# A chunked linear-attention step: the score tiles of the prompt heads reduced from eight to six

## What is computed

```python
def step(s, inp):                                   # one chunk of tokens, one state s per head
    qb, kb, vb, gb = inp
    G = jnp.cumsum(gb, axis=1)                      # log decay, per token and channel
    o_inter = jnp.einsum('bthk,bhkv->bthv', qb * jnp.exp(G), s)
    decay = jnp.exp(jnp.where(causal, G[:, :, None] - G[:, None, :], -jnp.inf))
    scores = jnp.einsum('bthk,btshk->btsh', qb, decay * kb[:, None])
    o_intra = jnp.einsum('btsh,bshv->bthv', scores, vb)
    ...
```

## Time and profile before

| | us |
|---|---|
| time, median of three runs | 1828.41 |
| the three runs | 1827.68, 1828.41, 1837.21 |
| the profiled execution, its own time | 1836.97 |
| its span (first to last instruction) | 1835.2 |

### The profile page before, as it was taken

How to read it: one execution, slowest core, us unless ns; L and a number is a source line. 1 busy time by engine, 2 the same in 40 slices (tenths; PEclk the granted TensorE clock), 3 DMA queues, 4 the chain that set the end, 5 groups by cost and what they waited for, 6 DMA issues and landing times.

```text
span 1835.2 us, 23214 instructions
## 1 busy us (share of the span) xinstructions
PE 1779.1 (97%) x9594; PEld 1549.2 (84%) x9594; DVE 1296.9 (71%) x1099; ACT 1036.0 (56%) x934; POOL 112.1 (6%) x101
## 2 busy tenths in 40 slices
PE   8999999999999998998999999999999999899997
PEld 7988888999999978886888878888788888788886
DVE  6635555444347345547988888888988888788897
ACT  4443224333334342227777777777777777677776
POOL 2011120000000011210400000000000000000200
PEclk9998879999999978788999999999999999999999
DMA  9458144443453512137999999999999999899994
GB/s 291 160 180 241 35 111 147 141 158 107 137 172 116 161 40 54 41 90 257 380 395 395 394 363 387 365 375 393 375 362 363 370 397 378 297 383 365 383 385 186
DMA packets 272616, 474.20 MB, mean 258 GB/s; under 512 B 41578, under 2 KB 103266, under 8 KB 272504
## 3 DMA queue, kind: packets, MB, share of 16 engines
q1 hardware_dynamic: 266432, 452.50, 69.5%
q10 hardware_dynamic: 3368, 12.75, 2.1%
q0 software_dynamic: 2704, 7.39, 1.4%
HBM read 454.82 MB, written 29.84 MB: 264 GB/s over the span
## 4 chain that ended last, share of the span: by engine, by line
PE 93%; DVE 4%; ACT 1%; issue 1%; DMA 0%; DVEq 0%; ACTq 0%
PE ps L1676 17%; PE ps L1677 17%; PE ps L2297 11%; PE ps L1671 9%; PE ps L1672 9%; PE ps L2318 5%; PE ps L1770 4%; PE ps L2183 3%; PE ps L1880 3%; PE ps L1865 2%; PE ps L2201 1%; PE ps L2336 1%; PE ps L1918 1%; PE ps L2145 1%; PE ps L2035 1%
## 5 line engine op out<-in xcount | busy, mean ns | idle before, releaser
L1556 DVE TENSOR_TENSOR spL<-ring,spH 128x2048 fp32r<-128x2048 f32 x336 | 767.3, 2292 | 111.2 <-ACT spH L954 106.4
L954 ACT ACTIVATE spH<-ring 128x2048 fp32r<-128x2048 f32 x336 | 643.4, 1917 | 136.3 <-PE ps L2297 74.0
L1676 PE MATMUL ps<-spH,XH 128*128 128x512 f32 x896 | 356.5, 398 | 1.9 <-issue 1.9
L1677 PE MATMUL ps<-spH,XL 128*128 128x512 f32 x896 | 352.5, 393 | 2.3 <-issue 2.3
L1037 DVE TENSOR_TENSOR spL<-ring,spH 128x2048 fp32r<-128x2048 f32 (+1 forms) x74 | 158.8, 2146 | 182.3 <-ACT spH L660 182.1
L1671 PE MATMUL ps<-hnH,spH 128*128 128x320 f32 x928 | 277.3, 313 | 4.1 <-DVE hnL L1052 2.2
L1672 PE MATMUL ps<-hnL,spH 128*128 128x320 f32 x928 | 275.6, 311 | 0.0
L2297 PE MATMUL ps<-spL,XH 128*128 128x512 f32 x896 | 242.5, 393 | 0.2 <-DVE spL L1556 0.2
L660 ACT ACTIVATE spH<-ring 128x2048 fp32r<-128x2048 f32 (+1 forms) x74 | 133.4, 1803 | 187.9 <-PE ps L2183 73.6
L1677 PEld LDWEIGHTS ps<-spH,XL 128*128 128x128 f32 x896 | 169.0, 189 | 38.4 <-issue 2.7
L2297 PEld LDWEIGHTS ps<-spL,XH 128*128 128x128 f32 x896 | 168.6, 188 | 38.6 <-DVE spL L1556 0.9
(11 more groups left out here) (358 smaller groups left out, 1944.0 us busy)
## 6 DMA issues: line engine op xcount, KB each, us to landing
ring<-in_w_exp_in_dram SPq DMA_DIRECT2D x224, 1024.0 KB, 8.1
ring<-in_w_exp_out_dram SPq DMA_DIRECT2D x112, 1024.0 KB, 8.5
ring<-in_w_in_dram SPq DMA_DIRECT2D x28, 1024.0 KB, 5.3
ring<-in_w_ffn_in_dram SPq DMA_DIRECT2D x22, 1024.0 KB, 5.1
token_rows<-token_rows ACTq DMA_DIRECT2D x1, 11776.0 KB, 41.9
ring<-in_w_ffn_out_dram SPq DMA_DIRECT2D x16, 704.0 KB, 4.6
ring<-in_w_out_dram SPq DMA_DIRECT2D x8, 1024.0 KB, 5.1
out_dram<-ring SPq DMA_DIRECT2D x32, 256.0 KB, 2.6
```

What stands on the lines that cost most here:

```text
L954: A(esplit(j)[0], src, ACT.Copy).then_inc(S("hi_done"), 1)
L1556: V.tensor_tensor(lo, eslot(j)[0], hi.bitcast(F32), ALU.subtract).then_inc(S("split_done"), 1)
L1676: mm(out, x[0], w, start=start, stop=False)
L1677: return mm(out, x[1], w, start=False, stop=False)
```

## The change

For the prompt tiles (t < 2) the two top levels, 5 and 6, no longer get tiles of their own. At level 6 there is one block of 64 keys by 64 queries in the whole tile, at level 5 there are two of 32 by 32, and these blocks do not overlap with one another or with the diagonal. `scores` now writes levels 0 to 4 as before and the plain product into the sixth tile; then one product with 64 columns of weights and 64 moving columns (level 6) and two with 32 and 32 (level 5, on output partitions 0 to 31 and 64 to 95) are written over their blocks of that sixth tile. The mask of the sixth tile is the diagonal plus the blocks of both levels. `masked` runs over 768 columns in place of 1024, and `output` accumulates six products in place of eight. What `exponents` and `products` make is the same. The constant table is 256 columns narrower, so the tensors behind it lie 1 KB lower in SBUF. The sample heads (t = 2) are as before.

```diff
@@ level_tables
     w[:, levels, :] = same & (i[:, None] <= i[None, :])
     m[:, levels, :] = np.eye(n)
+    if levels == LV:
+        m[:, LV - 2, :] += m[:, LV - 1, :] + m[:, LV, :]
+        m = m[:, :LV - 1, :]
@@ masked
-                    SCv = flat(SCb[h % 2])[:, 0:(nl + 1) * n]
+                    SCv = flat(SCb[h % 2])[:, 0:(nl - 1 if t < 2 else nl + 1) * n]
                     if t < 2:
-                        V.tensor_tensor(SCv, ps[:, 2:4, :].rearrange("p b n -> p (b n)"), tabv("mask"), ALU.mult
+                        V.tensor_tensor(SCv, ps[:, 2:4, :].rearrange("p b n -> p (b n)")[:, 0:(nl - 1) * n], tabv("mask"), ALU.mult
                                         ).then_inc(S("sc_done"), 1)
@@ scores
-                    for v in range(nl + 1):
+                    wide = nl - 2 if t < 2 else nl
+                    for v in range(wide + 1):
                         out = ps[0:n, 2 + (v * n) // 512, (v * n) % 512:(v * n) % 512 + n]
-                        if v < nl:
+                        if v < wide:
                             m = mm(out, flat(Ykb[h % 2])[:, v * n:(v + 1) * n],
                                    flat(Yqb[h % 2])[:, v * n:(v + 1) * n], start=True, stop=True)
                         else:
                             m = mm(out, kT[:, h, o:o + n], qT[:, h, o:o + n], start=True, stop=True)
+                    if t < 2:
+                        for v in (nl - 1, nl - 2):
+                            w = 1 << v
+                            for k in range(0, n, 2 * w):
+                                m = mm(ps[k:k + w, 2 + wide // 4, wide % 4 * n + k + w:wide % 4 * n + k + 2 * w],
+                                       Ykb[h % 2][:, v, k:k + w], Yqb[h % 2][:, v, k + w:k + 2 * w], start=True, stop=True)
                     m.then_inc(S("sc_mm"), 1)
@@ output
-                    for v in range(nl + 1):
+                    last = nl - 2 if t < 2 else nl
+                    for v in range(last + 1):
                         m = mm(out, vtk_of(t)[0:n, h * P:(h + 1) * P], flat(SCb[h % 2])[0:n, v * n:(v + 1) * n],
-                               start=v == 0, stop=v == nl and t != 1)
+                               start=v == 0, stop=v == last and t != 1)
```

## The result

The changed kernel takes 1810.89 us (median of four executions, 1807.6 to 1818.62) against 1830.88 for the kernel before (four executions beside it): the ratio is 0.9893, with a 95% interval of 0.9848 to 0.9937. That is 20 us, where 11.5 were forecast. A second set of executions gave the same: ratio 0.9895 (0.985 to 0.9939).

What follows compares the result with a forecast made beforehand. PE was taken to bound the kernel, busy for 97% of the span. Output 7.9, mask 2.5, scores 0.7 and shorter last pass 0.4 made 11.5 us, from the median 1828.41 to 1816.9 us; range 1809 to 1828.

Steps and rivals of the forecast that it cites:

- The bound, and that the gain arrives: Whole kernel: PE has 93% of the chain, engines hold back the experts' weight stream, so head savings arrive whole.
- Output: Prompt heads' output: four passes fewer in each of 16 heads, 0.46 us per head at full clock; 7.9 us taken.
- The question of the low stretches: Four outputs at the lower clock: 9.0 us saved if stretches keep their place in the work, 7.4 if their length.
- Mask: DVE mask step, 768 columns for 1024: 272 ns less, on the path in ten heads; 2.5 us, bounds 2.0 and 2.7.
- Scores: Prompt scores, six narrow passes for four wide: gain 0.05 us per head, 14 heads, 0.7 us, bounds +2.9 and -2.9.
- my row: Sample heads' products with 64 weight and 64 moving columns, 0.067 us per pass, taken as price of the narrow passes.
- the rival on switching: Scores: each of three width switches costs 0.25 us in 14 heads, 10.5 us, so 1827.4, no change; chance 0.17.
- the group that I took as lower bound: The trace's smallest passes, 64x64 at 226.21, 0.040 us each: six narrow score passes 0.24, a gain of 0.21.
- The shorter last pass: Scores' last pass before the mask: 224 ns against 279, 0.05 us sooner, 0.4 us over eight heads.
- The clock: Rival in the heads: three more low stretches of 1.7 us give 1822.0, as many fewer 1811.8; chance against it 0.12.
- DVE in PE's place: Rival in the heads: DVE's products or splits end last, losing output savings; 1818.7 or 1820.6 us; chance 0.05.
- Slower by small products that don't overlap: Rival in scores: narrow passes at 0.4 us each, 16.5 us slower, 1844.9; gain gone at 0.20 per pass; chance 0.06.

Runs made afterwards that it cites:

- `after_fill`: Changed kernel plus dense PE passes in three places per layer where PE waits in the heads; ratio 0.9894 to the kernel before, clock loss 53.2 us.
- `output_mask_only`: Kernel before with mask over 768 columns and output over six tiles, scores as before, level 6 and diagonal left out; ratio 0.9913 to the kernel before.
- `plain_first`: Changed kernel with the plain product and its three narrow ones ahead of levels 0 to 4; ratio 0.9913 to the kernel before, 1760.3 us at full clock.
- `before_fill`: Kernel before plus dense PE passes in three places per layer where PE waits in the heads; ratio 0.9926 to the kernel before, clock loss 52.2 us.

## Why the prediction was right, and where not

**The bound, and that the gain arrives.** Right. PE's chain has the gain, the experts wait for the engines as before, and the stages behind the heads give nothing back.

**The number.** The time lies in the forecast's range, but by two misses that pull apart: the work on the path fell by 8.1 us where 11.5 were forecast, and the clock, which was to give next to nothing, gave 12. That they met inside the range is luck; the mechanism that the forecast named has two fifths of the measured gain.

**Output.** Right: 0.46 us per head forecast at full clock, 0.44 to 0.45 measured, about 7.1 us in 16 heads. The question of the low stretches, where I took 7.9 between 7.4 and 9.0, was asked too small: they don't keep their place, they partly go. Four outputs ran in them before; in the changed kernel's profile those of (0,1) still do, those of (1,1) don't.

**Mask.** The duration is right (272 ns forecast, 266 measured). The number of heads is not: after the change the mask leaves the chain in two heads of five per layer, because PE's own work between scores and output now ends last there. I had seen that for one of them (744.63). About 1.6 to 2 us in place of 2.5.

**Scores.** The term was a gain of 0.05 us per head; PE's timeline says a loss of 0.13 to 0.19, some 2 us in 14 heads. The experiments don't settle the sign in the whole time: -1.0 +- 0.6 and +1.0 +- 1.0 us at full clock, +0.3 and +1.9 in the head stages. The passes themselves are as cheap as my row (0.058 for 64 columns, 0.067 with the first step in it), and the four of 32 columns are cheaper still, since they run two by two. What is missing is the switches, about 0.1 us each: going in, from 64 to 32 columns, and going out. In the rival on switching I had taken the right mechanism with too high a price (0.25 each, three times), and dismissed it by a row that averages two switches over 16 passes (0.2 / 16 = 0.012 per pass can hardly be seen in 0.064) and whose passes move 128 columns. The trace of the kernel before had the price of going in, at the group that I took as lower bound:

```profile
225.93 0.28 PE L1961 MATMUL ps<-tabR,La 128*128 128x128 f32 x1
226.14 0.27 PE L1996 MATMUL ps<-M,xdt 64*64 64x64 f32 x2
```

Here 0.21 us pass from the last 128-column pass to the first 64-column one, 0.1 more than the 0.112 of a dense stream. The shorter last pass is there (213 ns on the mean for 32 columns against 279), 0.07 us for the mask where 0.05 were forecast. The Trainium skill (TensorEngine Tiling (Array Packing), Key Properties) says that a change of tiling mode drains TensorE. The runs agree that a switch costs time, and show the price here: about 0.1 us, a third of a lone pass; whether TensorE is empty in it no row shows.

**The sum.** Output 7.1, mask about 2, scores between 0 and -2.5: 6.5 to 9 us, and 8.1 +- 0.8 were measured at full clock. The forecast was 11.5: 0.8 too much for the output, some 0.5 to 1 for the mask, 1 to 3.5 for the scores with their shorter last pass. I had expected the head stages shorter by 5 to 6 us each; they are by 5.4 and 8.1, of which about 3.5 each is work.

**The clock.** This is what brought the result below the forecast, and the step that was weakest: the sum gave it next to nothing (7.9 in place of 7.4 for the output), because I couldn't read its direction. I named it as a rival with the same price in both directions and 1811.8 us for three low stretches fewer, and gave a chance of its own only to the bad one. The measured 1810.89 is the good one. The runs show that it isn't chance: all sets of kernels with eight output tiles and no filled waits, or one, have mean losses of 62.0 to 70.0 us (six sets, 10 to 28 executions each), and all sets with six output tiles 44.8 to 58.3 (eight sets, 4 to 11 executions). The means don't overlap, though the nearest two lie only 3.7 us apart; single executions do. One place where it happens in both layers of these two profiles is the output of (1,1). Before, in layer 0 (start, us, passes):

```profile
196.30 3.78 PE L1880 MATMUL ps<-SC,vtk 128*128 128x128 f32 x16
```

Changed:

```profile
195.09 1.60 PE L1891 MATMUL ps<-SC,vtk 128*128 128x128 f32 x12
```

What PE did before it fell there was two rounds of sample-state products (L1914 with 8 moving columns, L1918 with 64 rows), in both kernels alike. The place isn't fixed: in the profile of `after_fill` the output of (1,1) in layer 1 takes 2.93 us again (from 710.66), and that of `output_mask_only` in layer 0 as well (from 194.42). Why the shorter outputs ahead of them leave the clock at its upper level isn't settled. Filling the waits in the kernel before has the same effect on the loss, so it isn't the shorter output as such that is needed; a rule that would have told me the direction beforehand doesn't follow from these runs.

**DVE in PE's place** did not happen as a loss; it is seen only as the masks that left the chain. **Slower by small products that don't overlap** did not happen: 0.64 us for the six in a dense stream is 0.107 each, switches and all, where it decides from 0.20. It is just under the 0.11 at which I had said I would be wrong.

## What to carry to other kernels

Split the time into span times granted clock and the rest, execution by execution, before judging a change of half a per cent: the mean of the first part over 10 executions is good to 1 us here and shows the edit; the second scatters by 10 us from one execution to the next, its means over a set by up to 7, and it can itself be the larger half of an edit's effect. Price small matrix products by their group, with what stands before and behind, and not by the mean pass of a long run of them: six passes of 0.058 us or less cost 0.5 to 0.6 with their switches, at least as much as the four wide ones. And where PE is the bound and its waits are known, a few dense passes in them are an experiment worth one run: in the kernel before they gave 13 us, in the changed kernel nothing, and in one wait alone nothing.

## What the runs showed of the hardware that was not expected

Between products of 128, 64 and 32 weight columns each change of width costs about 0.1 us at the upper clock level: 0.32 against 0.22 us going in (708.88 to 709.20), 0.15 against 0.06 from 64 to 32 (709.31 to 709.46), 1.22 against 1.11 for the ten wide passes behind (`plain_first`).

Two products of 32 weight columns whose outputs lie on other partitions run side by side: their four passes start two at 709.46 and two at 709.51.

The spread between executions of the kernel before, 1821.9 to 1848.65 us, is in the main the granted clock's: at 0.972 and 0.956 the full-clock times are 1769.1 and 1765.5.

A stage without any changed instruction, the Mamba-2 part of layer 1, went from 47.1 to 42.1 us because of what ran before it: its clock is 0.74 in one kernel and 0.82 in the other, and 0.82 again when only waits were filled ahead of it (`before_fill`, 42.2 us).
